# Twelve up panels whose matmuls read the 256 tokens in another order

## The reference

```python
def conv_glu_ffn(h, w_up, conv_w, conv_b, w_down):
    u = h @ w_up                     # 256 x 1024 by 1024 x 5632
    u = lax.conv_general_dilated(u, conv_w[:, None, :], window_strides=(1,), padding=[(CONV_W - 1, 0)],
                                 dimension_numbers=('NWC', 'WIO', 'NWC'), feature_group_count=2 * D_FF) + conv_b
    gate, up = jnp.split(u, 2, axis=-1)
    return (jax.nn.silu(gate) * up) @ w_down

        h = h + conv_glu_ffn(rmsnorm(h, ffn_norm[i]), ffn_up[i], ffn_conv[i], ffn_conv_b[i], ffn_down[i])
```

## Time and profile before

| what | value |
|---|---|
| runs, us | 989.7, 994.25, 995.42 (median 994.25) |
| profiled execution, us | 989.6 |
| its span from first to last instruction, us | 987.9 |
| granted TensorE clock, mean | 0.998 |
| PE busy, PE weight load busy | 98%, 88% |
| DVE, ACT, POOL busy | 68%, 58%, 15% |
| HBM read | 171.59 MB, 175 GB/s over the span |

### The profile page before, as it was taken

How to read it: one execution, slowest core, us unless ns; L and a number is a source line. 1 busy time by engine, 2 the same in 40 slices (tenths; PEclk the granted TensorE clock), 3 DMA queues, 4 the chain that set the end, 5 groups by cost and what they waited for, 6 DMA issues and landing times.

```text
span 987.9 us, 15443 instructions
## 1 busy us (share of the span) xinstructions
PE 969.1 (98%) x6186; PEld 868.2 (88%) x6186; DVE 672.5 (68%) x947; ACT 575.7 (58%) x807; POOL 147.9 (15%) x133
## 2 busy tenths in 40 slices
PE   8989999999999999999999999999999999999997
PEld 8978889999988888788999998888988899888886
DVE  5796468888854677876888885466555566844554
ACT  6767747666643676776665663356564466544433
POOL 5403202343410000000234330002000000000010
PEclk9999999999999999999999999999999999999999
DMA  9653266676575544436676665646645543555541
GB/s 296 204 171 130 84 171 183 186 199 195 190 276 194 186 161 165 140 117 171 186 199 183 183 202 173 210 129 207 224 139 170 161 159 129 169 190 196 187 165 53
DMA packets 159511, 173.66 MB, mean 176 GB/s; under 512 B 4110, under 2 KB 120320, under 8 KB 159440
## 3 DMA queue, kind: packets, MB, share of 16 engines
q1 hardware_dynamic: 157104, 167.00, 53.6%
q0 software_dynamic: 2160, 5.41, 1.8%
q10 hardware_dynamic: 176, 0.27, 0.1%
HBM read 171.59 MB, written 1.07 MB: 175 GB/s over the span
## 4 chain that ended last, share of the span: by engine, by line
PE 83%; DVE 6%; ACT 6%; issue 3%; DMA 1%; POOL 1%; POOLq 0%; ACTq 0%; DVEq 0%
PE bank L907 30%; PE bank L882 29%; PE bank L939 16%; ACT w_hi L1252 2%; PE bank L927 2%; DVE w_lo L1593 1%; PE bank L967 1%; PE bank L1041 1%; ACT le L1370 1%; DMA w_raw<-in_ab_w_in 1%; DVE x_lo L1607 1%; ACT L1370 1%; PE bank L987 0%; DVE le_s L1937 0%; ACT le_s L1517 0%
## 5 line engine op out<-in xcount | busy, mean ns | idle before, releaser
L1593 DVE TENSOR_TENSOR w_lo<-w_raw,w_hi 128x2048 fp32r<-128x2048 f32 x153 | 349.7, 2289 | 192.4 <-ACT w_hi L1252 192.2
L1252 ACT ACTIVATE w_hi<-w_raw 128x2048 fp32r<-128x2048 f32 x155 | 296.8, 1917 | 237.7 <-PE bank L907 104.0
L907 PE MATMUL bank<-x_hi,w_hi 128*128 128x256 f32 x720 | 203.7, 283 | 0.7 <-DVE w_lo L1593 0.6
L907 PE MATMUL bank<-x_hi,w_lo 128*128 128x256 f32 x720 | 201.5, 280 | 0.0
L907 PE MATMUL bank<-x_lo,w_hi 128*128 128x256 f32 x720 | 201.4, 280 | 0.0
L882 PE MATMUL bank<-w_hi,x_hi 128*128 128x512 f32 x352 | 139.8, 397 | 1.9 <-DVE kaT L1755 0.9
L907 PEld LDWEIGHTS bank<-x_hi,w_hi 128*128 128x128 f32 x720 | 135.6, 188 | 2.2 <-DVE w_lo L1593 0.8
L882 PE MATMUL bank<-w_hi,x_lo 128*128 128x512 f32 x352 | 137.2, 390 | 0.0
L882 PE MATMUL bank<-w_lo,x_hi 128*128 128x512 f32 x352 | 137.1, 389 | 0.0
L907 PEld LDWEIGHTS bank<-x_hi,w_lo 128*128 128x128 f32 x720 | 136.8, 190 | 0.0
L907 PEld LDWEIGHTS bank<-x_lo,w_hi 128*128 128x128 f32 x720 | 135.4, 188 | 0.2
(11 more groups left out here) (354 smaller groups left out, 1474.5 us busy)
## 6 DMA issues: line engine op xcount, KB each, us to landing
w_raw<-in_ffn_up SPq DMA_DIRECT2D x88, 512.0 KB, 5.1
w_raw<-in_w_in SPq DMA_DIRECT2D x35, 1024.0 KB, 5.2
w_raw<-in_ffn_down SPq DMA_DIRECT2D x22, 1024.0 KB, 5.0
w_raw<-in_ab_w_in SPq DMA_DIRECT2D x13, 1024.0 KB, 5.6
w_raw<-in_ple_gate SPq DMA_DIRECT2D x8, 1024.0 KB, 5.1
w_raw<-in_c_w_in SPq DMA_DIRECT2D x6, 1024.0 KB, 6.1
w_raw<-in_ab_w_out SPq DMA_DIRECT2D x4, 1024.0 KB, 5.0
w_raw<-in_w_mem_kv SPq DMA_DIRECT2D x4, 1024.0 KB, 6.3
```

The lines of the kernel that those rows point to most:

```text
L907: mm = pe.matmul(bank[b][:, c * 256:c * 256 + 256], wv[w][:, k, c * P:(c + 1) * P], x[:, k, :], start=(k == 0 and m == 0 and not (first an ...
L1252: act.activation(w_hi(n), raw[n % RAW][:, :], ACT.Copy).then_inc(*mark("weights_hi", ("hi", n)))
L1593: dve.tensor_tensor(w_lo(n), raw[n % RAW][:, :], plain(w_hi(n)), ALU.subtract).then_inc(*mark("weights_lo", ("lo", n)))
```

## The change

In the panels `i` = 8, 10, 12, 14, 16 and 18 of both up stages (12 of 44), the moving operand is read in another order of its tokens. The output columns in PSUM stay next to each other, so that the bank holds the tokens in this new order; the DVE instruction that scales the bank puts them back, by writing `conv_in` in the new order and reading the norms in it. It does so in two instructions of 256 columns, one for each `c`, instead of one of 512.

- panel 10: token 0, 2, 4, ... and then 1, 3, 5, ... (a step of 8 bytes)
- panel 8: 0, 128, 1, 129, ... (each token 512 bytes from its neighbour in the order)
- panels 18, 16, 12, 14: the two halves of the tokens in turn, by runs of 2, 4, 8 and 16 neighbouring tokens

```diff
+ORDERS = {8: ("p (h b c) -> p b h c", 1), 10: ("p (b h c) -> p h b c", 1), 12: ("p (h b c) -> p b h c", 8),
+          14: ("p (h b c) -> p b h c", 16), 16: ("p (h b c) -> p b h c", 4), 18: ("p (h b c) -> p b h c", 2)}
+TOKEN_ORDER = {FIRST[f"up{l}"] + i: v for l in range(2) for i, v in ORDERS.items()}
+
+def reordered(n, ap):
+    how, c = TOKEN_ORDER[n]
+    return ap.rearrange(how, h=2, c=c)
+
+def in_order(n, ap):
+    how, c = TOKEN_ORDER[n]
+    return ap.rearrange("p (b h c) -> p b h c" if how.endswith("b h c") else "p (h b c) -> p h b c", h=2, c=c)
...
-                            mm = pe.matmul(bank[b][:, c * 256:c * 256 + 256], wv[w][:, k, c * P:(c + 1) * P], x[:, k, :],
+                            out, moving = bank[b][:, c * 256:c * 256 + 256], x[:, k, :]
+                            if n in TOKEN_ORDER:
+                                out, moving = in_order(n, out), reordered(n, moving)
+                            mm = pe.matmul(out, wv[w][:, k, c * P:(c + 1) * P], moving,
...
-                    dve.tensor_tensor(conv_ins[l][i % 2][:, :, :], two(b), row2(NORM_OF[stage]), ALU.mult).then_inc(*mark("scaled", ("scaled", n), ev))
+                    if n in TOKEN_ORDER:
+                        for c in range(2):
+                            dst, row = reordered(n, conv_ins[l][i % 2][:, c, :]), reordered(n, ROWS[NORM_OF[stage]])
+                            dve.tensor_tensor(dst, in_order(n, two(b)[:, c, :]), row, ALU.mult).then_inc(*mark("scaled", ("scaled", n), ev))
+                    else:
+                        dve.tensor_tensor(conv_ins[l][i % 2][:, :, :], two(b), row2(NORM_OF[stage]), ALU.mult).then_inc(*mark("scaled", ("scaled", n), ev))
```

## The result

| | before | after |
|---|---|---|
| median of the runs compared, us | 991.98 (984.72 to 995.42, 4 runs) | 1006.68 (1006.37 to 1009.56, 4 runs) |
| profiled execution, us | 989.6 | 1009.56 |
| its span, us | 987.9 | 1007.8 |
| ratio | | 1.0164, 95% interval 1.0125 to 1.0203 |

A forecast was written before the change was run, and what follows sets the result against it. PE was taken to bound the kernel, never idle in the up stages. Panels 8, 10, 18 and the rest add 32.4 + 10.7 + 10.7 + 0 = 53.8 us to 994.25 us, giving 1048 us; range 992 to 1056 us.

The forecast's parts named there:

- What bounds: Both up stages: PE has practically no idle time, any slower matmul is paid in full, and down0 catches nothing up.
- A new 16 bytes costs some 1.8 ns: Reads of moving columns from SBUF: each new 16-byte line costs 1.77 ns on PE, 1.84 ns on DVE.
- If a line is fetched anew each time, a matmul takes 256 x 1.77 = 453 ns: Panel 8, both up stages: every column is in another line than the one before, adding 32.4 us.
- its sign, panel 8 below 10 us: Panel 8: a length below 10 us would show the forecast wrong on fetching anew; 21.8 us was expected in up0.
- The lower end given there: Panel 8: adds 0 if the engine keeps two lines at hand and takes the halves from them.
- The rival of 1005 us: Up stages: one pattern alone, panel 8 or panel 10, pays half rate, 10.7 us; chance 0.18.
- Panel 18: 227 ns, 10.7 us for both stages: Panel 18, runs of two: two columns of a line, then the other half's line, 227 ns a matmul, adding 10.7 us.
- Panels 12, 14, 16: 0: Runs of 8, 16 and 4 tokens: as many lines as before, each used whole, so 0 us added.
- DVE's additions hidden: Bank scaling in 12 panels: split 1.7 us together, hops up to 0.78 us a panel, all off the path.
- The Trainium skill's two rules: SBUF: two hits on a 16-byte line suffice for full rate; PSUM: access patterns with gaps slow matmuls significantly.
- The sum: All twelve reordered panels: 32.4 + 10.7 + 10.7 + 0 = 53.8 us added, giving 1048 us.
- The flip between two distances: Up stages: a reordered panel may switch plain matmuls between 113.4 and 117.8 ns, 3.0 us won or lost.

The follow-up runs named there:

- R: Account fitted to the pattern runs, not a run: kept lines are free; of lines new in one round the first is unseen, each further one costs 1.8 ns.
- the slowest group: Runs of the kernel before, nothing changed, stand in three groups at about 985, 989 and 994 us; this is the one at about 994 us.

## Why the prediction was wrong in size

- **What bounds.** Right. PE has no idle time in the up stages, each slower matmul was paid in full, and down0 caught nothing up.
- **A new 16 bytes costs some 1.8 ns.** Right as a number, wrong as to when. Panel 10's matmul was priced 227 ns and took 229; each stream then has a new line at every column, 128 x 1.79 ns. That the forecast had this panel right is in part luck: counted over the one sequence it also has 128 lines. 0 1 4 5 8 9 and, at 240 columns, every third column pay the same for a column of a stream. That the plain read stands at this limit agrees with the runs: with four columns of a line in a stream 512 columns fell from 227.5 to 215.8 ns, the time of the plain float32 matmul in the earlier trace rows.
- **Panel 8: "If a line is fetched anew each time, a matmul takes 256 x 1.77 = 453 ns", 32.4 us.** This is the step that failed, and its sign, panel 8 below 10 us, came up: 5.35 us. Measured 111.6 ns, 0.1 us less than a plain panel in up0 and 0.3 us less in up1. I had counted changes of line between neighbours in the sequence, as if one line were held; the runs show two streams, and each of them takes four columns of one line in succession. The lower end given there, that the engine keeps two lines at hand, is nearer to it. The rival of 1005 us (chance 0.18) had two branches; the one by which "only the step doubles the number of lines" had panels 8 and 10 right. Without panel 18 and the small prices of 12 to 16 it is this result.
- **Panel 18: 227 ns, 10.7 us for both stages.** Measured 170 ns, 2.71 + 2.50 = 5.2 us. The forecast gave it as many lines as panel 10. Per stream it has 64, as many as a plain panel and half of panel 10's, but they come in pairs that are used in turn. By R, which was fitted to this number among others, one line of each pair is paid: 32 x 1.8 = 58 ns over 112.
- **Panels 12, 14, 16: 0.** Measured 5.91, 5.78 and 6.09 us against 5.44 and 5.65 us: 1.5 us in up0 and 0.8 us in up1 together. Small, but not zero. The columns of a line follow each other as before, and the price falls with the number of jumps between the halves; why a jump costs anything is open, and R doesn't hold it.
- **DVE's additions hidden.** Right: alone they measured 1.0008. The prices were too high: the pair with hops of 512 bytes is 0.45 us over plain, the pair with a step of two and the plain pairs 0.07 us, where the split alone was given 0.14 us and the hops up to 0.78 us more.
- **The Trainium skill's two rules.** The Trainium skill, page "SBUF — State Buffer", section "Specifications (TRN2)", asks two hits on a line for the full rate. Read per stream the traces nearly agree: two successive columns of a line in each stream are a plain panel (113 or 118 ns), one is 229 ns. But two are not quite the full rate, since four are 111.6 ns, and at 512 columns 215.8 against 227.5 ns. Read over the whole sequence, as I read it, it fails both ways, for panel 8 (free) and for panel 10 (two hits, half rate). The Trainium skill, page "Advanced Engine Details and Errata", section "PSUM Cachelines", was not tried, since no matmul here writes with gaps; reading PSUM with gaps by DVE, which that section does not speak of, costs nothing here (691 ns).
- **The sum.** From profile to profile the twelve panels cost 9.7 us in up0 and 8.4 us in up1, 18.1 us where 53.8 were forecast. The failed step is 32.8 of these 35.7 us, panel 18 another 5.5; the 2.3 us of panels 12 to 16 and 0.2 of panel 10 go the other way. The two chains differ by 19.2 us. In up0 they differ by 2.2 us more than the patterns, since the plain panels up to 11 stood at 118 ns in this execution and at 113 ns in the one of before; in up1 by 1.0 us less, since most plain panels behind 12 stood at 113 ns, where they had been at 118. The medians differ by 14.7 us: the profiled execution after was the longest of its four, and two of the four runs of before were from the slowest group. Later runs of before have medians of 989.25 us (19 runs) and 985.05 us (11 runs), so the 14.7 us are rather too small, and the 18.1 us are the surer number.
- **The flip between two distances.** I gave it +-3.0 us. It is real: plain panels after a reordered one change from 5.44 to 5.65 us and back, and the kernel before has it between executions. A pattern can set the distance of the plain panels behind it. Without panel 10 the change's up0 begins at 5.44 us and its up1 at 5.65 us, and yet from panel 13 on the plain panels of both are alike: 5.46 us at 13, 5.66 at 15, 5.45 at 17. What picks the distance at the start of a stage is open.

Open: why three lines are kept and whether four fail by their number or by their addresses, why a further new line costs 1.8 ns only when another is new beside it, and why 64 bytes apart is 7 ns cheaper.

## What to carry to other kernels

Where PE is never idle, the order in which a matmul takes its moving columns is a lever by itself: count, for the even and the odd columns of the sequence apart, how many in succession lie in one 16-byte line (four of fp32r is best, two is plain, one is half speed). Taking the two halves in turn by single columns gave 1.5 to 5% per matmul, and it is paid only where the order is undone: undo it in the reader of PSUM, where a step of two was free, and not in the instructions that split the weights. Before pricing a pattern by the distance between neighbours, ask how many lines an engine can hold, and in how many streams it reads; a few patterns in one kernel tell.

## What the runs showed of the hardware

- A float32r matmul of 256 columns in storage order has two distances, 113.3 and 117.8 ns. In a stage of plain panels one of them holds throughout, and it differs between executions of the same program; behind a reordered panel it can change. With four columns of a line per stream it is 111.6 to 111.7 ns in every run here. With 512 columns it is 227.5 ns in storage order, and 215.8 to 216.5 ns with the halves in turn.
- The moving columns behave as two streams, the even and the odd ones of the sequence. Three lines in turn for a whole matmul (320 bytes apart) are 111.4 ns for 240 columns, four (256 bytes apart) 220 ns for 256.
- The cheapest pattern, one line used 16 times over, is no faster than 111.6 ns, where 256 columns at 2.4 GHz are 106.7 ns.
- Reading 2048 columns of SBUF with a step of two takes ACT 2.98 us instead of 1.92 and DVE 2.93 instead of 2.29. DVE's scaling of 256 columns pays nothing for a step of two on its SBUF sides (425 ns, plain 416) and 0.23 us for hops of 512 bytes (645 ns). Why the step costs in one and not in the other is open. A step of two on PSUM was free (691 ns for 512 columns).
